# Seven-product paired steps in the first down projection, and eight of them in the last two blocks of the last one

## What is computed

```
def conv_ffn(h, w_up, conv_w, conv_b, w_down):
    u = causal_depthwise_conv(h @ w_up, conv_w, conv_b)
    val, gate = jnp.split(u, 2, axis=-1)
    return (jax.nn.gelu(gate) * val) @ w_down
...
        x = x + conv_ffn(rms_norm(x, ffn_norm[layer]), ffn_w_up[layer], ...)
```

## Time and profile before

| | us |
|---|---|
| median of 3 runs (2265.86 to 2281.33) | 2266.58 |
| the profiled execution, its time | 2266.04 |
| its span | 2264.4 |
| PE busy | 2254.7 |
| DVE busy | 1559.0 |
| ACT busy | 1289.7 |
| POOL busy | 642.8 |

### The profile page before, as it was taken

One profiled execution on the slowest core, in us unless ns is written; L12 is line 12 of the kernel. 1 busy time (PEld: TensorE's weight loads), 2 busy tenths in 40 slices (PEclk: granted clock), 3 DMA queues, 4 the chain that ended last, 5 costly groups with the idle time before them and its releaser, 6 DMA issues.

```text
span 2264.4 us, 33777 instructions
## 1 busy us (share of the span) xinstructions
PE 2254.7 (100%) x11036; PEld 1902.6 (84%) x11036; DVE 1559.0 (69%) x1892; ACT 1289.7 (57%) x1692; POOL 642.8 (28%) x1051
## 2 busy tenths in 40 slices
PE   9999999999999999999999999999999999999999
PEld 7888888988888888888888888898888888888887
DVE  6766775676767667665556678758767667678666
ACT  6655664565556555554444777556656556555444
POOL 1720001234343343412221000215344343432100
PEclk9999999999999999999999999999999999999999
DMA  8656335546676776766665555646876676778876
GB/s 277 207 197 205 134 123 177 177 152 220 217 224 210 225 218 215 223 208 201 202 204 186 186 186 169 203 140 204 250 223 214 220 222 214 221 226 237 271 225 198
DMA packets 150694, 464.70 MB, mean 205 GB/s; under 512 B 26656, under 2 KB 27552, under 8 KB 150608
## 3 DMA queue, kind: packets, MB, share of 16 engines
q1 hardware_dynamic: 121152, 423.55, 57.1%
q0 software_dynamic: 29312, 39.95, 6.5%
q10 hardware_dynamic: 144, 0.06, 0.0%
HBM read 433.17 MB, written 2.10 MB: 192 GB/s over the span
## 4 chain that ended last, share of the span: by engine, by line
PE 96%; DVE 2%; ACT 1%; issue 1%; DMA 1%; POOL 0%; SPq 0%; ACTq 0%; DVEq 0%
PE ps L475 47%; PE ps L480 23%; PE ps L433 10%; PE ps L437 5%; PE ps L418 2%; PE ps L454 2%; PE ps L1003 2%; PE ps L1005 1%; PE ps L816 1%; PE ps L1108 1%; PE ps L802 0%; DVE w_lo L407 0%; PE ps L896 0%; POOL u_t L2343 0%; DMA u_t<-z_t 0%
## 5 line engine op out<-in xcount | busy, mean ns | idle before, releaser
L379 DVE TENSOR_TENSOR w_lo<-raw,w_hi 128x1024 fp32r<-128x1024 f32 x704 | 875.8, 1247 | 585.2 <-ACT w_hi L373 582.6
L373 ACT ACTIVATE w_hi<-raw 128x1024 fp32r<-128x1024 f32 x703 | 741.6, 1059 | 719.3 <-PE ps L480 599.0
L475 PE MATMUL ps<-w_hi,xg_hl 128*128 128x512 f32 (+1 forms) x3392 | 832.1, 387 | 2.1 <-DVE xg_hl L1604 2.1
L475 PEld LDWEIGHTS ps<-w_hi,xg_hl 128*128 128x128 f32 x3392 | 631.3, 188 | 131.3 <-DVE xg_hl L1604 2.0
L480 PE MATMUL ps<-w_lo,xg_hl 128*128 128x512 f32 (+1 forms) x1696 | 449.4, 387 | 0.0
L480 PEld LDWEIGHTS ps<-w_lo,xg_hl 128*128 128x128 f32 x1696 | 316.4, 188 | 65.3 <-DVE w_lo L379 0.4
L475 PE MATMUL ps<-w_hi,a_hl 128*128 128x512 f32 x1464 | 364.5, 391 | 0.3 <-ACT kmem_tok L1240 0.2
L2343 POOL DMA_DIRECT2D u_t<-z_t x704 | 347.6, 502 | 2.8 <-issue 2.8
L475 PEld LDWEIGHTS ps<-w_hi,a_hl 128*128 128x128 f32 x1464 | 272.8, 188 | 57.5 <-issue 0.7
L480 PE MATMUL ps<-w_lo,a_hl 128*128 128x512 f32 x732 | 195.8, 389 | 0.0
L433 PE MATMUL ps<-xg_hl,w_hi 128*128 128x512 f32 x512 | 161.7, 397 | 0.0
(11 more groups left out here) (247 smaller groups left out, 2101.1 us busy)
## 6 DMA issues: line engine op xcount, KB each, us to landing
raw<-in_w_stream SPq DMA_DIRECT2D x775, 512.0 KB, 4.1
u_t<-z_t POOLq DMA_DIRECT2D x704, 34.0 KB, 3.4
t_in<-in_w_stream SPq DMA_DIRECT2D x24, 256.0 KB, 3.4
t_in<-in_w_stream POOLq DMA_DIRECT2D x24, 256.0 KB, 7.5
raw<-in_w_stream SPq DMA_DIRECT2D x14, 256.0 KB, 4.9
bias<-in_rel_bias POOLq DMA_DIRECT2D x4, 768.0 KB, 6.2
memT<-in_mem_t POOLq DMA_DIRECT2D x4, 512.0 KB, 6.2
gate_w<-in_gate_w POOLq DMA_DIRECT2D x4, 512.0 KB, 3.9
```

The costliest lines, as they stand in the source:

```text
L373: nc.scalar.activation(w_hi[:, s, :], raw[:, s, :], ACT.Copy).then_inc(hi_done, 1)
L379: nc.vector.tensor_tensor(w_lo[:, s, :], raw[:, s, :], w_hi[:, s, :].bitcast(F), ALU.subtract).then_inc(lo_done, 1)
L475: nc.tensor.matmul(ps[:, bank + tt, 0:n], a[:, k0 + k, tt * P:tt * P + P], w_hi[:, s, k * n:k * n + n], start=start and k == 0 and q == 0, ...
```

## The change

Four edits, all in the order and the place of work; the result is the same sum.

- One table, `PAIR_ORDER`, in place of `LAST_ORDER`. Blocks 0 and 1 of **both** down projections now go by the same list: six ordinary pairs, then six paired steps (before: none in `down0`, where the blocks were done one after the other; in `down1` six after five ordinary pairs). Blocks 2 and 3 of `down1` have eight paired steps, with one ordinary pair between each two. Blocks 2 and 3 of `down0` stay as they were.
- For the steps in `down0` there is a second `t_in`, laid in the old `xg_hl`, and SP waits ahead of its first load until PE is done with all up units. `t_raw` has one buffer instead of two and lies where `z_t` lay.
- In `down0` blocks 0 and 1 end together. ACT copies bank 4, DVE makes nine additions in three parts (`pair_sums`), and the turns, moves and additions to `x` of blocks 0 and 1 come later, beside block 2. POOL's accumulating DMAs for the six steps stand at the head of its `down_section`.
- The activation sums have 3 rounds in `down0` and 4 in `down1` (for the units 0 to 7).

```diff
-LAST_ORDER = [[("c", u) for u in range(6, 11)] + [x for j in range(4) for x in (("s", j), ("c", 11 + 2 * j), ("c", 12 + 2 * j))]
-              + [("s", 4), ("c", 19), ("s", 5), ("c", 20), ("c", 21)],
-              [("c", u) for u in range(6, 9)] + [x for j in range(6) for x in (("s", j), ("c", 9 + 2 * j), ("c", 10 + 2 * j))] + [("c", 21)]]
-FORMS_AT = [0, 2, 10]
+PAIR_ORDER = \
+    [[("c", u) for u in range(6, 12)] + [x for j in range(4) for x in (("s", j), ("c", 12 + 2 * j), ("c", 13 + 2 * j))]
+     + [("s", 4), ("c", 20), ("s", 5), ("c", 21)],
+     [("c", u) for u in range(6, 12)] + [x for j in range(4) for x in (("s", j), ("c", 12 + 2 * j), ("c", 13 + 2 * j))]
+     + [("s", 4), ("c", 20), ("s", 5), ("c", 21)],
+     [("c", u) for u in range(8, 11)] + [x for j in range(8) for x in (("s", j), ("c", 11 + j))] + [("c", u) for u in range(19, 22)]]
+FORMS_AT = [[0, 2, 14], [0, 2, 14, 40][:LAYER_FORMS[1] // 2]]
...
+        t_in = [at("t_in0", XG + size([PAIRS[0], 4, 2, P]), [2, UE]), at("t_in1", FFN + 2 * size([4, 4, RUN]), [2, UE])]
+        t_raw = at("t_raw", ZT, [UE])
...
+            units(4 * SLOTS, first["down0"])
+
+            sp.wait_ge(pe_unit, first["down0"])
+            rec0 = first["rec"] - EXTRA
+            down_units(0, first["down0"], rec0 + SLOTS, list(range(PAIRS[0])))
...
+                pe.wait_ge(proj_free, fblock["down0"] + 2)
+                block_pair(0, value_there)
+                for n in (2, 3):
+                    pe.wait_ge(dn_out, TT * (n - 1))
...
+            def pair_sums(part):
+
+                if part == 0:
+                    dve.wait_ge(p1_out, 1)
+                    ch.link(dve, V.tensor_tensor(dn_sum[:, :], y_up[:, 0, :], ps[:, 6, :], ALU.add))
+                    ch.link(dve, V.tensor_tensor(dn_sum[:, :], dn_sum[:, :], ps[:, 7, :], ALU.add))
+                if part == 1:
+                    V.tensor_tensor(y_up[:, 0, :], y_up[:, 0, :], ps[:, 0, :], ALU.add).then_inc(dn_out, 1)
+                    V.tensor_tensor(y_up[:, 1, :], dn_sum[:, :], ps[:, 1, :], ALU.add).then_inc(dn_out, 1)
+                if part == 2:
...
+            def added(n):
+
+                z, x = n % 2, t_in[int(n >= PAIRS[0])]
+                pool.wait_ge(t_loaded[z], 32 * (n // 2 + 1))
+                for h in range(2):
+                    pool.dma_start(x[:, z, h * COLS:(h + 1) * COLS], t["w_stream"][RAW_OF[n] + 1, :, 0:COLS],
+                                   accum_op=ALU.add).then_inc(t_added[z], 16)
+
             def down_section():
+                for n in range(PAIRS[0]):
+                    added(n)
                 pool.wait_ge(ssq_ps, REC)
...
+                move(0)
+                move(1)
```

More of the change, by code:

```diff
@@ L369, in split_hi @@
             s = c % SLOTS
-            act.wait_ge(raw_full[s], times(16 * (c // SLOTS + 1), i, 16 * (per // SLOTS)))
+            before = EXTRA if c >= first["rec"] else 0
+            act.wait_ge(raw_full[s], times(16 * ((c - before) // SLOTS + 1), i, 16 * (per // SLOTS)))
             if c >= SLOTS:
@@ L990, in last_section @@
             def last_section():
-                c0 = first["down1"]
                 def value_there(k):
```

393 lines of the change are left out of this document (222 added, 171 removed).

## The result

| | before | after |
|---|---|---|
| median | 2266.77 (2265.67 to 2281.33, 6 runs) | 2284.26 (2283.09 to 2286.86, 6 runs) |
| the profiled execution, its time | 2266.04 | 2284.43 |
| its span | 2264.4 | 2282.8 |

A forecast was written before the change was run, and what follows sets the result against it. PE was taken as the bound, busy 2254.7 of 2264.4 us. 2266.0 - 5.4 - 1.6 (gains) + 19.2 (both holes) + 0.2 (handover) + 1 (loop) + 2 (clock) = 2281.4 us, predicted as 2281, range 2272 to 2289.

The forecast's parts named there:

- The gains: Eight ordinary pairs become paired steps, saving 5.44 us of PE; first paired step of `down1` loses its 1.55 us excess.
- Hole A: Start of `down0`: PE idles while SP waits for the last up unit, then issues four `t_in` loads first; 8.6 us.
- Hole B: First paired step of `down0`: PE waits for its low part, as POOL's accumulating DMAs stand behind `fconv`; 10.6 us.
- the 8 to 13: Expected trace sign: PE idle 8 to 13 us ahead of the low part in the first paired step of `down0`.
- The clock: TensorE's clock may fall after the idle stretches, slowing the paired step behind Hole B; 2 us, bounds 0 and 4.8.
- The rival that it stays low for longer: Restart behind Hole B at half clock costs all of 4.8 us; time 2284 and up, chance 0.07.
- The handover to block 2 of `down0`: Banks 0 and 1 must be read out before block 2; 0.2 us, ends 0 and 1.
- Blocks 2 and 3 of `down1`: The loop making `t_in` gets little slack as steps come closer and DMA share rises to 0.96; 1 us, ends 0 and 6.
- the cover of 2.2: Slack in the `t_in` loop of `down1`: data landed at + 16.6, weight sums must begin by + 18.8; 2.2 us.
- Only hole A: Value half not pushed back in `down0`, so Hole B is 4.2 us or less; time 2271 to 2275, chance 0.12.
- No hole: SP's wait ends early enough and POOL's DMAs are in time in `down0`; time 2259, 0.3% faster, chance 0.06.
- The loop as the bound: Each of six steps in blocks 2 and 3 of `down1` waits 1 to 2 us; time 2286 to 2292, chance 0.1.

The follow-up runs named there:

- raw_first: Changed kernel, but SP issues the first four down units' loads ahead of the four `t_in` loads, still after its wait; 2280.83 us, ratio 1.0066.
- wait_late: Changed kernel with SP's wait for the last up unit and the first `t_in` loads put ahead of the ninth down unit, not the first; 2270.10 us.
- both: Changed kernel with the edits of wait_late and pool_first together; 2264.61 us, ratio to before 0.9985.
- early_forms: best without its new list for blocks 0 and 1 of `down1`; 2259.95 us, ratio to before 0.9973.
- both_hand: both with two ordinary pairs, not one, between the last paired step of blocks 0 and 1 of `down1` and blocks 2 and 3; 2263.61 us.
- best: both plus fourth activation-sum round at position 22, both_hand's list, and `t_in` loads of `down1` blocks 2 and 3 one raw unit sooner; 2259.58 us, ratio 0.9967.
- best5: The same kernel as best, timed once more in five rounds; 2259.32 us, ratio to before 0.9965.
- pool_first: Changed kernel with POOL's accumulating DMAs for the first two paired steps of `down0` issued ahead of its wait for `fconv`; 2277.07 us, ratio 1.0048.
- pool_fill: pool_first with 34 matmuls nobody reads, issued by PE while it otherwise stands idle ahead of `down0`; 2277.24 us, ratio to before 1.0043.
- both_forms: both with the fourth round of activation sums of `down1` at position 22 instead of 40; 2262.64 us, ratio to before 0.9978.

## Why the prediction was right, point by point

- **The gains.** In `down0` 6 x 0.68 = 4.08 was predicted, 4.05 came. In `down1` 1.36 and 1.55 were predicted, and both are there: the first paired step has no wait in the kernel after. The pace of the earlier trace rows is the whole price.
- **Hole A** was put at 8.6 (ends 6.2 and 10.9), measured 8.76. Term by term: issue of the loads 1.8, measured 1.81; landing 5.7, measured 5.6; copy 1.1, measured 1.15. The middle between two bounds was luck in its last digit, but both bounds came from rows whose queues were known, and raw_first shows the lower one (3.3) as it is.
- **Hole B** was put at 10.6 (4.2 to 12.9), measured 6.16, also below the 8 to 13 that the prediction named as its sign. With T the start of `down0`: z_t at T + 9.4 predicted, T + 9.1 measured (985.99); convolution T + 25.3, T + 24.9; last low part T + 33.2, T + 32.8; accumulating DMAs T + 34.2, T + 33.7; landed T + 41.6, T + 40.1; PE's low part T + 44.2, T + 42.7. The chain is 1.5 us shorter: 0.5 ahead of the DMAs and 1.0 from their issue to the sums. The 7.4 counted for that was the start of DVE's sums in `down1`, where DVE was in a convolution until then; the two DMAs had landed 7.0 behind the issue there and landed 6.3 behind it here. The other 2.9 of the 4.4 is that PE wanted the part later, at T + 36.5 and not at T + 33.6: the slow matmuls behind hole A. They are in the table as a loss of their own, but as the prediction said they cost nothing: without them hole B would be 9.1.
- **The clock** was put at 2 behind B (0 to 4.8), measured 2.16, a middle between two bounds and so luck in its closeness. The rival that it stays low for longer did not come.
- **The handover to block 2 of `down0`**: 0.2 predicted, at most 0.03 measured.
- **Blocks 2 and 3 of `down1`**: 1 us (0 to 6), measured 1.5. The mechanism was right: the engines' share went from 0.84 to 0.93 in 2198 to 2232 (0.96 predicted), and the landings grew with it. The kernel after, its SP and POOL timelines, against the earlier trace rows:

```profile
2214.99 0.33 SPq L632 DMA_DIRECT2D t_in<-in_w_stream  x1
...
2221.09 1.78 POOL L2445 DMA_DIRECT2D t_in<-in_w_stream  x2 [9.10 <-DMA t_in<-in_w_stream]
```

```profile
2230.20 0.69 DVE L2110 TENSOR_TENSOR t_raw<-t_in,raw 128x512 f32<-128x512 f32 x1 [3.96 <-DMA t_in<-in_w_stream]
```

  From the load to POOL's DMA were 4.43 us and are 6.10, and the sums begin 15.2 behind the load, where 12.6 was counted: 2.6 more eats the cover of 2.2. The seven other profiles with this loop have 0 to 4.3 us, so that the nearness of 1 and 1.5 is partly luck.
- **What the prediction left out** are two waits in `down1`: the fourth round of activation sums at position 40, which the diff shows and to which no price was put (1.6 us), and the handover from blocks 0 and 1 to 2 and 3 of `down1` with x_tok (1.6). Together 3.2, and the sum, 2281.4, fell short of the profiled 2284.4 by 3.0. The other differences nearly cancel: hole B and the clock together 1.3 less than the sum had, hole A 0.2 more, the loop 0.5 more, the handover in `down0` 0.2 less, and 0.6 more in the part ahead of `down0`, which nothing in the change explains: up to there the fourteen profiles lie between 967.06 and 968.81, and the kernels don't differ. That the sum came within 3 us owes something to errors of both signs.
- **The rivals.** Only hole A: no, B was there, and it is partly an echo of A: 3.6 alone (wait_late), 9.1 behind A. No hole: no. The loop as the bound: its mechanism is real, but it cost 1.5 us, where the rival needed 6 to 12. The prediction held the forecast too small to be told from no change; the interval of the measured ratio, 1.0046 to 1.0092, tells it. That none of the holes comes from the paired steps is shown by both: with two places moved in queues the first down projection has all of its gain.

What makes x_tok late can be read from the traces, though no kernel was built to test it. ACT's and DVE's timelines of the kernel after, ahead of PE's start at 2166.26:

```profile
2163.20 1.06 ACT L424 ACTIVATE w_hi<-raw 128x1024 fp32r<-128x1024 f32 x1 [3.20 <-DMA raw<-in_w_stream]
```

```profile
2165.43 1.28 DVE L2074 TENSOR_TENSOR x_tok<-x_tok,ps 128x512 f32<-128x512 f32 x2
```

PE may not write a bank of block 2 before DVE has added what is in it to `x_tok`, and in program order the addition shown, for the second unit of block 2, stands behind the low part of a unit of weights that landed late. In all nine profiles with the list of the kernel after, this addition starts 2.2 us behind ACT's copy of that unit, and PE, where it waits, 0.8 us behind its start. So what decides is when the unit lands, counted from the start of block 2 (1.0 us behind it here, 0.4 ahead of it in early_forms, where PE does not wait), and not how long ACT has waited for it. With the list of both_hand and best the addition for the second unit no longer waits for such a unit, but the one for the first still can (1.36 us in both_hand, 0.4 in best5, none in best). Open is why the unit lands later in some executions than in others.

## What to carry to other kernels

Price a new wait by everything that stands behind it in its queue, and follow it on: SP's wait was on one thing (the place of `xg_hl`), but the first unit of the stream stood behind it, and POOL's DMAs stood behind a load for the other layer, with which they have nothing to do. When the arithmetic saving is a few us, the place of two waits in a queue can be worth more than the saving (here 19.7 us against 7), and moving them brings it back. Go through every table in a diff, also the positions that seem to be bookkeeping: the round at position 40 cost 1.6 us, more than the 1.4 that two more paired steps gave.

## What the runs showed of the hardware

- TensorE's clock fell to 0.50 in or behind rests that are short beside a kernel: with a rest of 8.8 us it cost 2.96 in the kernel after, with 9.0 us 1.46 in pool_first, with 4.7 us 1.49 and with 7.4 us 2.4 (both raw_first), with 3.6 us 1.55 (wait_late), with 6.2 us 2.16. In pool_fill rests of 2.0 us and of 2.2 us (at x_tok) cost 1.8 and 1.7; in both_forms one of 2.2 us, at 2212.3, left it at 1.00. The price was 1.5 to 3 us each time or none; it did not grow in step with the rest. At the lower level matmuls of 512 columns follow each other at 0.43 us, at the higher at 0.227.
- The accumulating DMAs of 256 KB landed in 3.6 to 11.8 us, with a median of 6.8 to 7.5 in each of the fourteen profiles, and the plain loads of `t_in`, of the same size, in 2.5 to 8.8, with medians of 3.4 to 4.1. The Trainium skill (DMA: Bandwidth & Descriptors, "Anatomy of one DMA — SWDGE (gpsimd) path") would have an estimated 2.6 for a GpSimd DMA of that size; the quickest accumulating one here took 3.6.
- A DMA share of 0.99 in a stretch of the loop (best) went with no wait of PE in blocks 2 and 3, 0.93 (after) with waits that cost 1.5 us over the loop: how full the engines are did not tell, and with the load issued 4 us earlier none of four profiles has a wait of the loop left.
